# Expert stage of a streaming encoder layer: rows turned once and kept in SBUF, three raw weight slots, the turn of the hidden layer inside the next expert's matmuls

## What is computed

```python
def step(acc, xs):
    wg, wu, wd, c = xs                       # (1024,256), (1024,256), (256,1024), weight of each frame
    hdn = jax.nn.silu(t @ wg) * (t @ wu)
    return acc + c[:, None] * (hdn @ wd).astype(jnp.float32), None
acc, _ = lax.scan(step, acc0, (w_gate, w_up, w_down, combine.T.astype(t.dtype)))
```

## Time and profile before

| | us |
|---|---|
| median of 3 runs | 1424.16 |
| lowest and highest | 1421.84, 1424.8 |
| span of the profiled execution, first to last instruction | 1420.8 |
| PE busy | 1264.7 (89%) |
| DVE busy | 796.2 (56%) |
| ACT busy | 616.8 (43%) |
| POOL busy | 67.5 (5%) |

### The profile page before, as it was taken

One profiled execution on the slowest core, in us unless ns is written; L12 is line 12 of the kernel. 1 busy time (PEld: TensorE's weight loads), 2 busy tenths in 40 slices (PEclk: granted clock), 3 DMA queues, 4 the chain that ended last, 5 costly groups with the idle time before them and its releaser, 6 DMA issues.

```text
span 1420.8 us, 22301 instructions
## 1 busy us (share of the span) xinstructions
PE 1264.7 (89%) x8549; PEld 1130.7 (80%) x8549; DVE 796.2 (56%) x938; ACT 616.8 (43%) x819; POOL 67.5 (5%) x132
## 2 busy tenths in 40 slices
PE   5989999999999999999989989982788888888880
PEld 4989999999999999999989989982455555555550
DVE  4437374473755736547365444326567677677645
ACT  5434243343433434335343222232566666666632
POOL 0001010010100101001010000003000000000002
PEclk9999999999999999999999999965799999999995
DMA  5261121211121112121102235533888888888836
GB/s 186 95 208 54 58 71 61 72 47 61 65 67 56 61 61 65 53 71 61 63 22 80 80 103 164 211 136 127 293 319 322 321 323 325 316 329 328 313 126 220
DMA packets 49434, 212.80 MB, mean 150 GB/s; under 512 B 5920, under 2 KB 8496, under 8 KB 37104
## 3 DMA queue, kind: packets, MB, share of 16 engines
q1 hardware_dynamic: 41200, 194.05, 39.2%
q0 software_dynamic: 2928, 10.05, 2.1%
q10 hardware_dynamic: 5264, 8.13, 1.6%
HBM read 181.25 MB, written 30.96 MB: 149 GB/s over the span
## 4 chain that ended last, share of the span: by engine, by line
PE 78%; DVE 7%; ACT 6%; DMA 4%; issue 3%; POOL 1%; SPq 0%; ACTq 0%; DVEq 0%; POOLq 0%
PE proj L620 25%; PE proj L1337 15%; PE wideB L1358 6%; PE proj L987 5%; PE wideA L378 4%; PE proj L930 3%; PE wideB L370 3%; PE wideB L384 2%; PE wideA L1324 2%; DVE xbl L1426 2%; ACT xbh L1422 2%; PE small L987 2%; DMA wraw<-in_w_in 1%; PE small L1178 1%; POOL scr_rows L1783 1%
## 5 line engine op out<-in xcount | busy, mean ns | idle before, releaser
L620 PE MATMUL proj<-xnh,whi 128*128 128x288 f32 x1152 | 347.9, 302 | 11.1 <-DVE xnl L1868 6.3
L620 PE MATMUL proj<-xnl,whi 128*128 128x288 f32 x1152 | 347.2, 301 | 0.0
L620 PE MATMUL proj<-xnh,wlo 128*128 128x288 f32 x1152 | 347.0, 301 | 0.0
L620 PEld LDWEIGHTS proj<-xnh,whi 128*128 128x128 f32 x1152 | 217.9, 189 | 12.3 <-issue 5.7
L1414 DVE TENSOR_TENSOR elo<-eraw,ehi 128x4096 fp32r<-128x4096 f32 x64 | 214.6, 3354 | 19.8 <-ACT ehi L1404 19.8
L620 PEld LDWEIGHTS proj<-xnl,whi 128*128 128x128 f32 x1152 | 217.8, 189 | 0.0
L620 PEld LDWEIGHTS proj<-xnh,wlo 128*128 128x128 f32 x1152 | 217.8, 189 | 0.0
L1337 PE MATMUL proj<-ehi,xbh 128*80 128x512 f32 x256 | 111.0, 433 | 33.9 <-DVE xbl L1426 33.9
L632 DVE TENSOR_TENSOR wlo<-wraw,whi 128x1024 fp32r<-128x1024 f32 x72 | 95.1, 1321 | 58.1 <-ACT whi L628 57.1
L1404 ACT ACTIVATE ehi<-eraw 128x4096 fp32r<-128x4096 f32 x32 | 116.1, 3627 | 0.5
L1337 PE MATMUL proj<-elo,xbh 128*80 128x512 f32 x256 | 109.9, 429 | 0.0
(11 more groups left out here) (329 smaller groups left out, 2370.2 us busy)
## 6 DMA issues: line engine op xcount, KB each, us to landing
wraw<-in_w_in SPq DMA_DIRECT2D x72, 512.0 KB, 3.3
eraw<-in_w_gate SPq DMA_DIRECT2D x32, 1024.0 KB, 4.9
eraw<-in_w_up SPq DMA_DIRECT2D x32, 1024.0 KB, 7.2
eraw<-in_w_down SPq DMA_DIRECT2D x32, 1024.0 KB, 5.5
wraw<-in_w_out SPq DMA_DIRECT2D x24, 512.0 KB, 3.7
xb<-scr_rows SPq DMA_DIRECT2D x32, 320.0 KB, 6.0
scr_y<-yout SPq DMA_DIRECT2D x32, 320.0 KB, 5.7
scr_gate<-gate ACTq DMA_DIRECT2D x16, 288.0 KB, 2.1
```

Of the source, the lines that this page charges most:

```text
L620: mm = pe.matmul(out, w[:, kc, :], x[:, kc, hh * HALF:(hh + 1) * HALF], start=(j == 0), stop=(j == 23))
```

## The change

**Rows.** The list no longer goes to SBUF in pieces of 80 rows. Its 9 tiles of 128 rows are loaded once (512 KB each, through three buffers `staged`), turned by TensorE at the start of the stage, and copied out of PSUM by ScalarE (even tiles) and VectorE (odd tiles) into one array `xT` in SBUF that holds all 1152 columns. Expert 0's gate/up matmuls stand between the turn of tile 0 and the other eight. GpSimd then takes the 80 columns of each expert out of `xT` (`rows_taken`, a copy into `xg`) and makes their low part (`rows_low`), both new work for it; the high part stays with ScalarE, now from SBUF.

**Weights.** There are three raw slots in place of two, and the low parts overwrite the raw ones, so that a slot is loaded again when the matmuls of its expert have read it, and not when the split has. The split is cut into gate, up and down of 2048 columns each. Three slots are filled ahead of the stage, the gate and up parts between the weights of the output projection.

**Turn of the hidden layer.** It moves behind the first 12 gate/up matmuls of the next expert, and the 12 down matmuls move behind its last 12. The loops over experts are written out (but for GpSimd's), and the orders of ScalarE, VectorE and SP are new. The 32 experts, their blocks of 80 and the arithmetic are the same.

```diff
-        def expert_tensor(pe, b, k, first=False, last=False):
-            if last:
-                down(pe, b - 1, 1 - k)
-            gate_up(pe, b, k, None if first or last else lambda: down(pe, b - 1, 1 - k))
-            if not last:
-                rows_turned(pe, b + 1, 1 - k)
-            hidden_turned(pe, b, k)
...
         def phase4_tensor(pe):
...
+            rows_turned(pe, 0)
+            pe.wait_ge(route, ROUTE_STEPS)
+            gate_up(pe, 0, 0, 0)
+            for t in range(1, TILES_S):
+                rows_turned(pe, t)
+            pe.wait_ge(xt_dve, TILES_S // 2)
+            for b in range(1, EXPERTS):
+                gate_up(pe, b, b % 2, b % RAW, lambda: hidden_turned(pe, b - 1, (b - 1) % 2))
+                down(pe, b - 1, (b - 1) % 2, (b - 1) % RAW)
+            b = EXPERTS - 1
+            hidden_turned(pe, b, b % 2)
+            down(pe, b, b % 2, b % RAW)
...
         def phase4_scalar(act):
...
+            for b in range(1, EXPERTS):
+                k = b % 2
+                if b > 1:
+                    silu_gate(act, b - 1, 1 - k)
+                    y_copy(act, b - 2, k)
+                if b + 1 < EXPERTS:
+                    gate_high(act, b + 1)
+                hidden_high(act, b - 1, 1 - k)
+                if b + 1 < EXPERTS:
+                    up_high(act, b + 1)
+                    rows_high(act, b + 1, 1 - k)
+                down_high(act, b)
...
+        def rows_taken(pool, b, k):
+            first = pool.value_load(table[0:1, at(b)], min_val=0, max_val=SLOTS)
...
+            if not (isinstance(b, int) and b < 2):
+                pool.wait_ge(e_xl, b - 1)
+            pool.tensor_copy(xg[k][:, :, :], xT[:, :, at(first, BR)]).then_inc(e_xg, 1)
+
+        def rows_low(pool, b, k):
+            pool.wait_ge(e_xg, b + 1)
+            pool.wait_ge(e_xh, b + 1)
+            if not (isinstance(b, int) and b < 2):
+                pool.wait_ge(e_gu, b - 1)
+            pool.tensor_tensor(xbl[k][:, :, :], xg[k][:, :, :], xbh[k][:, :, :].bitcast(F32), ALU.subtract)\
+                .then_inc(e_xl, 1)
...
-            with sp.Fori(KC + 1, KC + KC // 2) as j:
+            for q in range(2 * KC + 2, 3 * KC, 2):
                 for k in range(2):
-                    out_load(2 * j + k, k)
+                    out_load(q + k, k)
+                slot = q // 2 - KC - 1
+                gate_up_load(slot, slot, e_w[slot])
...
+            for t in range(TILES_S):
+                if t > 2:
+                    sp.wait_ge(nx["turned"], UNITS + t - 2)
+                sp.dma_start(staged[t % 3][:, :], scr_rows[t * P:(t + 1) * P, :]).then_inc(x_in[t % 3], 16)
+
+            for b in range(EXPERTS):
+                slot = b % RAW
+                if b + RAW < EXPERTS:
+                    sp.wait_ge(e_gu, b + 1)
+                    gate_up_load(b + RAW, slot, e_w[slot])
+                if b > 0:
+                    y_store(b - 1, (b - 1) % 2)
+                if b + RAW < EXPERTS:
+                    sp.wait_ge(e_dn, b + 1)
+                    down_load(b + RAW, slot, e_wd[slot])
```

More of the change, by code:

```diff
@@ L206, in encoder_layer, with place @@
         AT_MIX = AT_ML + BRANCH
-        EW = 24 * DE
-        AT_P3 = EW
+        GU = 16 * DE
+        DW = 8 * DE
+        def place(name, start, shape, dt=F32):
+            ctx = area(start)
+            t = sb(ctx, name, shape, dt)
+            ctx.close()
+            return t
         a2 = area(AT_YA)
@@ L772, in encoder_layer @@
         spread_rows = sem("spread_rows")
-        e_w, e_wd = [sem("e_w0"), sem("e_w1")], [sem("e_wd0"), sem("e_wd1")]
-        e_x = [sem("e_x0"), sem("e_x1")]
-        e_high, e_low, e_xt, e_xh, e_xl, e_gu, e_silu, e_hid, e_ht, e_hh, e_hl, e_dn, e_y = (
-            sem("e_" + k) for k in "high low xt xh xl gu silu hid ht hh hl dn y".split())
+        e_w, e_wd = ([sem(f"e_w{n}{k}") for k in range(RAW)] for n in ("gu", "d"))
+        xt_dve = sem("xt_dve")
+        e_hig, e_hid_w, e_log, e_lod, e_xg, e_xh, e_xl, e_gu, e_silu, e_hid, e_ht, e_hh, e_hl, e_dn, e_y = (
+            sem("e_" + k) for k in "hig hiw log lod xg xh xl gu silu hid ht hh hl dn y".split())
         e_out = [sem("e_out0"), sem("e_out1")]
-        o_x, o_w = sem("o_x"), sem("o_w")
+        o_w = sem("o_w")
         f_x = sem("f_x")
@@ L1157, in phase3_scalar @@
                     act.activation(tT[c % 2][:, :], wide(c)[:, :], ACT.Copy).then_inc(nx["copied"], 1)
-            for part in range(2):
-                weights_high(act, 0, 0, part)
+            gate_high(act, 0)
+            up_high(act, 0)
+            down_high(act, 0)
             act.wait_ge(route, R_GAP)
@@ L1380, in phase4_tensor @@
         def phase4_tensor(pe):
-            rows_turned(pe, 0, 0)
-            expert_tensor(pe, 0, 0, first=True)
-            expert_tensor(pe, 1, 1)
-            with pe.Fori(1, EXPERTS // 2 - 1) as i:
-                for k in range(2):
-                    expert_tensor(pe, 2 * i + k, k)
-            expert_tensor(pe, EXPERTS - 2, 0)
-            expert_tensor(pe, EXPERTS - 1, 1, last=True)
-            down(pe, EXPERTS - 1, 1)
+            rows_turned(pe, 0)
+            pe.wait_ge(route, ROUTE_STEPS)
@@ L1394, in further @@
[L1394 removed]
+                gate_up(pe, b, 0, 0)
                 hidden_turned(pe, b, 0)
[L1396 removed]
+                down(pe, b, 0, 0)
             further_blocks(pe, further)
[L1400 to L1409 removed]
@@ L1429, in silu_gate @@
+        def rows_high(act, b, k):
+            act.wait_ge(e_xg, b + 1)
+            wait(act, e_gu, b - 1)
+            act.activation(xbh[k][:, :, :], xg[k][:, :, :], ACT.Copy).then_inc(e_xh, 1)
         def silu_gate(act, b, k):
```

345 lines of the change are left out of this document (176 added, 169 removed).

## The result

The changed kernel took 1366.17 us (median of four runs, 1359.26 to 1369.27), the kernel before 1424.48 us beside it: a ratio of **0.9578**, 95% interval 0.9548 to 0.9608, so 4.2% faster. The forecast was 1365. The total agrees to 1 us, but its terms don't: the expert stage gained 17 us less than forecast, and a stage that the forecast left unchanged was 11 us shorter. The profiled execution has a span of 1367.6 us and a time of 1369.27, the longest of the four.

What follows compares the result with a forecast made beforehand. The chain through PE and the two turns between experts was taken to bound the kernel. 1031.3 + 2.3 + 30 x 9.3 + 14.3 = 1326.9 for the last store, span 1361.6, plus 3.4: 1365 us; range 1343 to 1404.

Steps and rivals of the forecast that it cites:

- PE's floor, 8.9 us: TensorE per expert at full clock: 8.4 us of matmuls plus 0.47 for the hidden turn.
- The clock: Expert stage: with the 2.65 us gap cut to well under 1, the granted clock stays up, near 1.00.
- The slower rival: Late-weight waits reach PE and lower the clock for whole experts; one in three gives 12.1 us, 1449; chance 0.07.
- GpSimd against DVE, 0.4 us: Copy and subtraction contend with DVE's low parts; PE loses 0.4 us per expert, making the pace 9.3.
- the rival at 10.3: DVE and GpSimd in full series at long prices, 7.58 + 2.75 = 10.3 us per expert, 1396; chance 0.14.
- That just fits: Down and next gate/up loads need 10.0 us; ACT asks for them after 10.3, so no wait.
- The sign that I had named for it: PE waits ending with a DMA landing would show the forecast wrong, pointing to the 322 GB/s rival.
- The DMA rivals: DMA rate stays at the expert stage's 322 GB/s: 3.474 MB take 10.8 us per expert, 1410; chance 0.12.
- The start: Expert stage: expert 1's gate/up starts at 1031.3, 17.0 us later than before, plus 2.3 for the low clock.
- The end, 14.3, and the rest, 34.7: From expert 31's gate/up to the last store 14.3 us; the 34.7 us behind that store stay.
- The router stage as before: Ahead of the expert stage: nothing changes, first row load issued at 997.17 as before.
- The 6.3 MB between the output projection's loads: Expert weights loaded ahead there, costed at nothing; one late tile would cost 4.9 us.

Runs made afterwards that it cites:

- the run with TensorE always busy: Against the kernel with gate/up loads asked for ahead, the rows' low part goes from GpSimd back to DVE; pace 8.52 us per expert, median 1339.37 us.
- the second profile: The changed kernel run and profiled once more, unchanged; pace 9.56 us per expert, median 1369.80 us.
- the three parts added: Changed kernel plus gate/up loads ahead, low rows on DVE, all tiles turned first with expert 1's weight split between tile copies; median 1330.65 us.

## Why the prediction was right, and where it was not

That the total was right within 2 us is luck: the pace cost 16.4 us more than forecast, the router stage gave back 10.75 and the place of the median 4.8. Inside the pace, too, errors offset each other: the floor was 0.3 us too high (8.58 in place of 8.9, the last step left out), GpSimd 0.2 too cheap (0.57 in place of 0.4), and late weights, at nothing in the forecast, cost 0.7. What the change moves on each engine came as forecast; the loads did not. Point by point:

- **PE's floor, 8.9 us.** Right in kind, a little high: with nothing late the gate/up group of 24 matmuls and the hidden turn take 5.8 us and the down group 2.8 in the run with TensorE always busy, which has 8.52. I carried the hidden turn at 0.47 as it stood behind a wait; among matmuls it costs 0.19.
- **The clock.** Right: 0.99 to 1.00 in the stage against 0.94. The gaps of 2.65 us are gone. The slower rival fell: waits for weights of up to 3.4 us on ACT reached PE as up to 2.6 us (3.1 on its weight loads), and the clock stayed up.
- **GpSimd against DVE, 0.4 us.** The idle came out: 0.41 to 0.46 before each group in the experts where nothing else is late; what it costs in pace is a little more, 0.57 (9.15 against 8.58, above). So did the sign that was to show it, low parts above 2.28 where GpSimd runs (3.56 for the down weights). Its copy took 0.72 alone (0.9 forecast) and its subtraction 1.53 to 1.54 (1.25). But under contention each takes 2.8 to 3.3, twice to four times its price, which the sum of durations in series (the rival at 10.3) did not describe: most of the lock lies beside other work. The Trainium skill, "SBUF — State Buffer", section "Who interferes with whom", says that the two exclude each other for whole instructions, and that the one issued first decides who is blocked; the trace agrees: the subtraction of 1029.20 ends at 1032.19, which is 1.43 us after DVE's low part of up is done (1028.47 + 2.29), nearly its 1.53 alone; and the low part of down, at 1030.90, takes 3.43, 1.14 above 2.29, while that subtraction still has 1.29 to go.
- **"That just fits"**, the loads. This is the step that failed. I set 7.6 us of transfer and 2.4 of latency, 10.0, against 10.3 from issue to need. Counted as there, from the issue of the down weights, up lands after 11.9 us at the median (10.2 to 13.7, issues from 1060 to 1290); after its own issue after 11.1, and up to 12.9. The store that SP had issued ahead of the three loads lands only 2.8 us after the down weights' issue (median): the 10.0 had no term for it (no run leaves the store out, so its part of the lateness is argued). And ACT needed both halves before it could begin with gate. What the store costs can't be had from the share: 0.94 x 9.87 less 7.58 leaves 1.70, near the upper bound of 1.78, but the same sum for the run with the low rows on DVE (1.01 x 8.58) leaves 1.09, about the lower bound of 1.12. A fit with 0.3 us to spare, between two numbers each uncertain by more than that, should have been costed as a wait in part of the experts: 0.7 us each in this profile (0.5 in the second), 9.85 in place of 9.3 with the two errors above, 16.4 us in all. The sign that I had named for it (PE's waits ending with a landing) appears one step removed, on ACT.
- **The DMA rivals.** The stage at 322 GB/s fell. The rate follows demand: 355 in the changed kernel, 379 and 404 in the faster ones.
- **The start.** Expert 1's gate/up came 18.3 us later after the first issue than before, against 17.0 forecast, and 19.6 against 19.3 with the low clock; found in the same place, with the loads of tiles 4 to 8 in the chain as worked out.
- **The end, 14.3, and the rest, 34.7.** Right within 0.2.
- **The router stage as before.** Failed, and could not be foreseen from one profile: the stage has two durations, 10.6 us apart, in one and the same program. Without that the profiled span would have been 1378.
- **The 6.3 MB between the output projection's loads.** No price is to be seen: the first turn of the router begins at 938.90, 941.87 and 935.52 in three profiles of the kernel before, and at 933.73 to 942.26, 939.1 at the median, in ten of the changed one and its variants.

The stage itself, from first row load to last store, was to go from 388.96 to 329.7 us; it went to 346.62 and, in the second profile, 340.48. The change does what it says, and leaves 42 to 48 us in its own stage (298.33 with the three parts added), which came from the order of SP's queue, the order at the start and one operation put back on DVE.

## What to carry to other kernels

When the pace of a loop falls, recompute when each load is asked for, not only how many bytes it moves: a load that stood behind another engine's group and a store was late here by 0.5 to 0.7 us per expert, and issuing it at the moment its buffer came free gave all of it back. A vector operation that is moved to GpSimd to relieve DVE can cost more there than in series on DVE, if DVE works on two SBUF operands most of the time: count the time under contention (3.0 us here against 0.82). And before a difference of two single profiles is put down to a change, compare the stages that the change doesn't touch.

## What the runs showed of the hardware

- The busy share of the DMA engines is not a rate: 0.94 stood at 355 GB/s, 1.00 at 374, 379 and 389 and 1.01 at 404 GB/s, all with the same transfers. A share of 1.00 did not mean that no more could be moved.
- GpSimd's copy of 128x640, with one operand in SBUF, took 0.72 us alone and, beside DVE's low parts, 1.2 to 2.8 at the mean, by its place among them.
- The router stage ran at a granted clock of 0.50 for 25.36 us in some executions and at 0.90 in others of one and the same program, although TensorE was busy in the slower form too (from 945 to 960 for 15.00 of 15 us in the kernel before, for 14.09 in the changed kernel's second profile). What decides between the two was not tried.
